# Weighted V of an even and an odd head in one block of matmuls, on the two halves of the array's columns

## What is computed

```python
def dense_causal_attention(q, k, v):
    ...
        s = jnp.einsum('bhqd,bhkd->bhqk', qi, k, preferred_element_type=jnp.float32) * scale
        s = jnp.where(kpos[None, :] <= qpos[:, None], s, -jnp.inf)
        p = jax.nn.softmax(s, axis=-1).astype(v.dtype)
        return jnp.einsum('bhqk,bhkd->bhqd', p, v)
```

## Time and profile before

| | |
|---|---|
| median of three runs | 943.77 us (943.41 to 944.41) |
| the profiled execution | 944.41 us, its span 942.3 us |
| mean granted TensorE clock | 0.992 of full speed |
| busy in the span: PE, DVE, ACT | 898.9 us (95%), 696.2 us (74%), 502.5 us (53%) |
| head loop of layer 0 | about 179.8 to 241.2 us |
| head loop of layer 1 | about 640.1 to 699.9 us |
| L825, layers and heads together | 64 records, 390 ns in the middle |
| L827 | 64 records, 273 ns |

### The profile page before, as it was taken

One profiled execution on the slowest core, in us unless ns is written; L12 is line 12 of the kernel. 1 busy time (PEld: TensorE's weight loads), 2 busy tenths in 40 slices (PEclk: granted clock), 3 DMA queues, 4 the chain that ended last, 5 costly groups with the idle time before them and its releaser, 6 DMA issues.

```text
span 942.3 us, 12772 instructions
## 1 busy us (share of the span) xinstructions
PE 898.9 (95%) x5020; PEld 765.5 (81%) x5020; DVE 696.2 (74%) x1111; ACT 502.5 (53%) x726; POOL 27.8 (3%) x51
## 2 busy tenths in 40 slices
PE   8999989898999999999989998989899999999998
PEld 5788879776987888888868997988689778888886
DVE  5987899688797667685679967986858865575454
ACT  5554977356448443443473569844464763443441
POOL 0010000000000000000001000000000000000000
PEclk9999999999999999999999999999999999999999
DMA  9979825314643857777538973360244556555451
GB/s 376 391 289 382 318 90 179 134 46 179 268 171 142 311 209 270 280 281 281 201 132 340 364 269 134 135 223 2 90 182 179 184 180 230 208 191 187 158 179 45
DMA packets 29581, 198.12 MB, mean 210 GB/s; under 512 B 3281, under 2 KB 3793, under 8 KB 7506
## 3 DMA queue, kind: packets, MB, share of 16 engines
q1 hardware_dynamic: 23474, 155.22, 44.4%
q0 software_dynamic: 5760, 41.95, 11.6%
q10 hardware_dynamic: 288, 0.14, 0.1%
HBM read 196.24 MB, written 1.05 MB: 209 GB/s over the span
## 4 chain that ended last, share of the span: by engine, by line
PE 56%; DVE 29%; ACT 8%; issue 4%; DMA 3%; DVEq 0%; ACTq 0%
PE bank L573 13%; PE bank L575 13%; PE bank L574 13%; DVE w_lo L1352 10%; PE bank L534 3%; PE bank L535 3%; PE bank L536 3%; DMA raw<-in_slabs_dram 3%; DVE score L1544 2%; ACT w_hi L987 2%; DVE acc L1662 2%; DVE front L1359 1%; DVE score L1601 1%; PE bank L922 1%; ACT acc L1234 1%
## 5 line engine op out<-in xcount | busy, mean ns | idle before, releaser
L1352 DVE TENSOR_TENSOR w_lo<-raw,w_hi 128x2048 fp32r<-128x2048 f32 (+2 forms) x146 | 316.6, 2172 | 128.1 <-ACT w_hi L987 126.8
L987 ACT ACTIVATE w_hi<-raw 128x2048 fp32r<-128x2048 f32 (+2 forms) x146 | 264.3, 1811 | 146.8 <-PE bank L575 92.0
L573 PE MATMUL bank<-w_hi,h_hi 128*128 128x512 f32 x536 | 211.3, 394 | 8.2 <-DVE w_lo L1352 5.2
L575 PE MATMUL bank<-w_lo,h_hi 128*128 128x512 f32 x536 | 209.2, 390 | 0.0
L574 PE MATMUL bank<-w_hi,h_lo 128*128 128x512 f32 x536 | 208.9, 390 | 0.0
L573 PEld LDWEIGHTS bank<-w_hi,h_hi 128*128 128x128 f32 x536 | 100.6, 188 | 34.2 <-DVE w_lo L1352 7.7
L575 PEld LDWEIGHTS bank<-w_lo,h_hi 128*128 128x128 f32 x536 | 100.6, 188 | 21.4
L574 PEld LDWEIGHTS bank<-w_hi,h_lo 128*128 128x128 f32 x536 | 100.7, 188 | 20.3
L534 PE MATMUL bank<-h_hi,w_hi 128*128 128x256 f32 x384 | 112.3, 292 | 1.0 <-DVE w_lo L1352 1.0
L535 PE MATMUL bank<-h_lo,w_hi 128*128 128x256 f32 x384 | 109.0, 284 | 0.0
L536 PE MATMUL bank<-h_hi,w_lo 128*128 128x256 f32 x384 | 108.9, 283 | 0.0
(11 more groups left out here) (203 smaller groups left out, 1321.3 us busy)
## 6 DMA issues: line engine op xcount, KB each, us to landing
raw<-in_slabs_dram SPq DMA_DIRECT2D x124, 1024.0 KB, 4.9
front<-in_ada_dram POOLq DMA_DIRECT2D x29, 1024.0 KB, 5.6
acc<-in_ada_dram POOLq DMA_DIRECT2D x11, 1024.0 KB, 7.9
raw<-in_slabs_dram SPq DMA_DIRECT2D x16, 552.0 KB, 7.9
front<-in_ada_dram SPq DMA_DIRECT2D x5, 1024.0 KB, 11.3
raw<-in_slabs_dram SPq DMA_DIRECT2D x6, 768.0 KB, 6.9
proj<-in_ada_dram SPq DMA_DIRECT2D x2, 1024.0 KB, 9.2
x_t<-in_x_dram SPq DMA_DIRECT2D x2, 512.0 KB, 4.7
```

The source lines that it names most:

```text
L573: nc.tensor.matmul(o, hh, wh, start=first, stop=False)
L575: return nc.tensor.matmul(o, hh, wl, start=False, stop=final)
L987: nc.scalar.activation(w_hi[:, n % RING, 0:w], raw[:, n % RING, 0:w], ACT.Copy).then_inc(hi_ready.sem, 1)
L1352: nc.vector.tensor_tensor(w_lo[:, n % RING, 0:w], raw[:, n % RING, 0:w], w_hi[:, n % RING, 0:w], ALU.subtract).then_inc(lo_ready.sem, 1)
```

## The change

PE's `weigh_v` now takes a pair instead of a head. It is called in even steps from 4 on, for pair (n-4)/2: the odd head's V stays in the step where it was, the even head's V moves one step later, next to it. Inside, the four matmuls of two heads alternate: keys 0 to 127 of the even head, of the odd head, then keys 128 to 255 of the even head, of the odd head. Each head writes its own 64 partitions of the bank as before. There is one wait for ACT's copy, that of the odd head, where there were two.

Since an even head's transposed exponentials wait longer for their use, `pt_sb` has four places instead of two, in `acc` columns 1536 to 3071 (the indexer's `relu_b`, finished by then, had the same columns). ACT's copy now waits for V four heads back. Scores, transposes, banks, gate slabs and the order on DVE are as they were.

```diff
-        pt_sb = [acc[:, 2304 + 384 * i:2304 + 384 * (i + 1)] for i in range(2)]
+        pt_sb = [acc[:, 1536 + 384 * i:1536 + 384 * (i + 1)] for i in range(4)]
...
-                def weigh_v(n):
-                    kind, h = HEADS[n]
-                    at = {"a": P * h + A_NOPE, "b": C_BV + HD * h, "c": C_CV + HD * h}[kind]
-                    pair = n // 2
-                    if n % 2 == 0 and pair >= 2:
+                def weigh_v(pair):
+
+                    if pair >= 2:
 
                         pe.wait_ge(y_lo_done.sem, y_lo_done.at(l, pair - 1))
-                    pe.wait_ge(pt_out.sem, pt_out.at(l, n + 1))
-                    r, y = HD * (n % 2), bank[2 + pair % 2]
-                    nc.tensor.matmul(y[r:r + HD, 0:T], proj[:, 0, at:at + HD], pt_sb[n % 2][:, 0:T],
-                                     start=True, stop=False, skip_group_check=True)
-                    nc.tensor.matmul(y[r:r + HD, P:T], proj[:, 1, at:at + HD],
-                                     pt_sb[n % 2][:, T:T + P], start=False, stop=True,
-                                     skip_group_check=True).then_inc(pv_done.sem, 1)
+                    pe.wait_ge(pt_out.sem, pt_out.at(l, 2 * pair + 2))
+                    y, at = bank[2 + pair % 2], []
+                    for n in (2 * pair, 2 * pair + 1):
+                        kind, h = HEADS[n]
+                        at.append({"a": P * h + A_NOPE, "b": C_BV + HD * h, "c": C_CV + HD * h}[kind])
+                    for e in range(2):
+                        nc.tensor.matmul(y[HD * e:HD * (e + 1), 0:T], proj[:, 0, at[e]:at[e] + HD],
+                                         pt_sb[(2 * pair + e) % 4][:, 0:T], start=True, stop=False,
+                                         skip_group_check=True)
+                    for e in range(2):
+                        nc.tensor.matmul(y[HD * e:HD * (e + 1), P:T], proj[:, 1, at[e]:at[e] + HD],
+                                         pt_sb[(2 * pair + e) % 4][:, T:T + P], start=False, stop=True,
+                                         skip_group_check=True).then_inc(pv_done.sem, 1)
...
-                    if n >= 3:
-                        weigh_v(n - 3)
+                    if n >= 4 and n % 2 == 0:
+                        weigh_v((n - 4) // 2)
...
-                        if n >= 4:
-
-                            act.wait_ge(pv_done.sem, pv_done.at(l, n - 3))
-                        nc.scalar.activation(pt_sb[n % 2], bank[6 + n % 2][:, 0:P + T], ACT.Copy)\
+                        if n >= 6:
+
+                            act.wait_ge(pv_done.sem, pv_done.at(l, n - 5))
+                        nc.scalar.activation(pt_sb[(n - 2) % 4], bank[6 + n % 2][:, 0:P + T], ACT.Copy)\
                             .then_inc(pt_out.sem, 1)
```

## The result

| | median of 5 runs, us | lowest to highest | profiled execution: time, span |
|---|---|---|---|
| before, same job | 944.41 | 943.41 to 944.61 | 944.41, 942.3 |
| after | 948.62 | 948.11 to 949.23 | 948.24, 946.2 |

The ratio is 1.0047, 95% interval 1.0032 to 1.0062: slower by 4.2 us where 0.8 was forecast, and above the 947.3 at which the range ended. Lines of the changed kernel: V's two matmuls of a pair are L827 and L831, the maximum L1666, the normalisation L1677, ACT's copy of a head L1250, its y_hi L1255.

The account below looks back on a forecast made before the run. VectorE and ScalarE were taken to bound steps 0 to 11, TensorE step 12 and the last steps. Terms +0.10, +0.05, -0.87, +1.2 and +0.3 gave +0.8 on 943.77: 944.6 us, range 942.6 to 947.3.

Parts of the forecast that it names:

- pair's V block: TensorE's four V matmuls of two heads: halves overlap almost fully, 0.84 us with 0.05 for loading weights; bounds 0.79 and 1.44.
- steps 0 to 11, clock apart: Head loop's first twelve steps, where TensorE waits for VectorE: cheaper V gains the loop nothing.
- step 12, a layer: Pair (8, 9) stands where V(9) stood and still waits for ScalarE's copy of head 9: +0.05 us each layer.
- end of layer 0: Last loop steps of layer 0: the pair now waits for ScalarE's copy of head 15, +0.05 us.
- end of layer 1: Steps 13 to 18 of layer 1: V(12) leaves step 15, so gate slab and turn(15) come earlier, -0.87 us.
- (b): Steps 6 to 7, both layers: longer pause before scores(8) drops the clock, +0.15 us a layer, bounds 0 to 0.5.
- rival 2: Clock also falls at step 11, slowing step 12's gate slab: +1.5 us a layer, 946.1 or 947.6; chance 0.16.
- (a): End of layer 0's loop: pause before turn(15) drops the clock for V and gate slab, +1.2 us (0.5 to 2.2).
- rival 3: In every pair's V block the halves run one after the other: block 1.44 us, +2.4, time 946.4; chance 0.11.
- Rival 1: The clock stays up in the head loops despite longer pauses: -0.7 us, time 943.1; chance 0.20.
- Rival 4: TensorE bounds the head loop more than the chain shows; a third of 11.8 us saved gives 940.7; chance 0.05.

Follow-up runs that it names:

- e6: The changed kernel with filler matmuls on TensorE at the end of steps 6, 7, 11 and, in layer 0, 16: 942.94 us, ratio 0.9988 to before.
- e9: e6 with both heads of a pair on the same half of the array's columns: 945.98 us, ratio 1.0016 to before.
- e3: The kernel before with four places for transposed exponentials instead of two, V still head by head: 943.03 us, ratio 1.0000 to before.
- e2: The kernel before with most of the even heads' V matmuls left out: 946.47 us, ratio 1.0022 to before.
- e4: The changed kernel with both V matmuls of the even head issued first, then both of the odd head: 946.64 us, ratio 1.0034 to before.
- e10: The changed kernel with filler matmuls in two TensorE pauses outside the head loops: 945.73 us, ratio 1.0018 to before.
- e5: e6 without the fillers at step 16 of layer 0: 945.13 us, ratio 1.0004 to before.
- e1: The changed kernel with filler matmuls at the end of steps 6, 11 and, in layer 0, 16: 944.27 us, ratio 1.0007 to before.
- e8: The kernel before with filler matmuls in two TensorE pauses outside the head loops: 941.46 us, ratio 0.9970 to before.

## Why the prediction was wrong

It forecast 944.6, inside 942.6 to 947.3; the run gave 948.62. The mechanisms held, the clock's fall after longer pauses among them; the clock's price did not. Sorted by its own steps, with e6 to take the clock out:

| step of the prediction | forecast | measured |
|---|---|---|
| pair's V block | 0.84 (0.79 to 1.44) | 0.80 |
| steps 0 to 11, clock apart | 0 | 0.00 to 0.01 (e6, scores(13)) |
| step 12, a layer | +0.05 | +0.10, +0.09 |
| end of layer 0 | +0.05 | +0.10 |
| end of layer 1 | -0.87 | -0.83 |
| clock, (b), layer 0 and 1 | +0.15, +0.15 | +0.50, +1.63 |
| clock at step 12 | 0 (rival 2: +1.5) | +1.50 in layer 0, none in layer 1 |
| clock, (a) | +1.2 (0.5 to 2.2) | +2.66 |

The last three rows are after minus e6. They sum to 6.3 where the prediction had 1.5; the rows above them give -0.53 where it had -0.72.

**The block** went to the lower end of its bounds. Loading the second half's weights costs 0.01 at most, where 0.05 was taken. The Trainium skill ("TensorE: Matmul & The Clock Gate", Part 3) has a weight load overlap matmuls in flight only in other row groups. Here both halves use all 128 rows, and 0.80 against e9's 1.42 says that halves of the columns overlap as well; the measurement decides. So rival 3 is out, and the size that it gave to its mechanism, +2.4, is near e9's 1.21 + 1.35 = 2.6.

**Layer 1's end** came as worked out: the gate slab of step 15 stands straight behind turn(13), and turn(15) behind DVE's normalisation. After minus before goes from 1.73 at scores(14) to 0.81 at turn(15). The 0.05 too much at each pair that waits for ACT is there because V starts 0.61 after ACT's copy starts instead of 0.52 (e6 220.27 and 220.88, before 219.92 and 220.44).

**Pauses.** Both were foreseen: 3.36 us before scores(8) where the text said 2.7 to 3, 2.84 before turn(15) where it said 3.0. The clock fell at both.

**The step that failed is the price of a fall.** It was taken from the earlier trace rows as 3.4 us at 1.2 GHz, a loss of at most 1.7. Three of after's four falls in the loops lasted 6.8. One trace of before didn't show that length; the trace of e3, with the same code outside the loops, has it at 124.1 to 130.9, where before's lasted 3.4, so a second execution could have shown it. The bound of 2.2 for (a) had "if it stays low longer" in it, but only by 0.5. At (a) V, the gate slab of step 18 and the start of the branch products are all on PE's path, so most of the 6.8 us counted: 2.66, of at most 3.4. At (b) a slack of 1 us was set against a loss of 1.7 at most. What a fall there costs goes by its moment: in eight loops one of 6.8 us begins near scores(8), and they differ so (e2 against before, the others against e6):

| kernel, layer | clock falls at | scores(8) starts | cost by scores(13) |
|---|---|---|---|
| e4, 1 | 662.1 | 663.17 | 0.42 |
| after, 0 | 199.1 | 200.05 | 0.50 |
| e10, 1 | 661.5 | 662.24 | 0.55 |
| e4, 0 | 201.3 | 201.68 | 0.72 |
| e2, 1 | 662.9 | 663.22 | 0.82 |
| e10, 0 | 200.8 | 199.68 | 1.35 |
| after, 1 | 666.7 | 664.98 | 1.63 |
| e2, 0 | 202.1 | 200.22 | 1.71 |

Where it falls before the wait is over, a part of the low stretch passes over an idle PE; where it falls a microsecond or more after, all of it lies on work. The later it fell, counted from scores(8), the dearer it was, in all eight. No row of before could have told the moment, so with a stretch of 6.8 us (3.4 lost) the bounds of (b) should have been 0 and 3.4 less the slack, 2.4, instead of 0 and 0.5 (the dearest measured is 1.71). Moment matters at (a) too: in e5 the clock fell at 235.4, before turn(15), and cost 2.4; in after at 236.7, with turn(15), and cost 2.66.

**The second error is of the kind of case.** Rival 2, the fall at step 12, happened in layer 0 (219.6 to 223.0), at the place and with the price of +1.5 that it had. It was set up as another case than the forecast, with 0.16, when it is one more fall beside (a) and (b). In e1, e5, e6 two fillers stand there and nothing falls; of the kernels with pairs and without fillers, after has it in layer 0, e4 in layer 1, e10 in neither. So at this place it comes in some executions. Added up with the measured prices from the same job's median of before: 944.41 - 0.53 + 6.3 = 950.2, or 948.7 without the 1.5 of step 12; the median of after is 948.62. Its profiled execution had the 1.5, and the 1.7 of the fall at 170 was absent in it.

**The rest.** Rival 1 is e6 by its condition, if by fillers: 0.7 under before forecast, 0.12% (1.1 us) under it measured, with an interval of 0.01% to 0.22%. Rival 4, PE as the bound, is out by the marks up to scores(8).

What stays open: why a fall lasts 3.4 us in one place and 6.8 in another is seen only as the pattern of e10's halves, with the exception named there; no run varied it alone. In which executions step 12 falls, and at which moment a fall begins, is not explained.

## What to carry to other kernels

Where another engine sets the pace, taking work from TensorE can cost time: look at what its busy share becomes in the stretch before the next work that is on the path, and price a fall of the clock there by all of the path's matmuls that lie in it, for the longest low stretch that several traces of the kernel show (one of before showed only the shorter) and at its least favourable moment. Several such places are to be added, not weighed against each other. If the pause can't be avoided, a few matmuls into a free bank are cheap: 13 in the first loop and 8 in the second (e6) turned a loss of 0.47% into a gain of 0.12%.

## What the runs showed of the hardware

- fp32 matmuls with 64 columns each on the two halves of the array's columns, all 128 rows in both, run at once: 0.80 us a pair, 1.42 on the same half, 0.81 when issued head by head (e4). In e4 matmuls on one half start before matmuls on the other half that were issued ahead of them.
- Less work can be slower by the clock alone: e2 leaves out some 9 us of matmuls and takes 0.22% longer.
- The clock can fall without a long pause: in e1 after waits of 1.44 and 0.99 us with short work between and around them; in e8 after one of 1.16, without the change.
- The low stretches came in two lengths, 3.4 and 6.8 us (but for one at the very end of each trace); the trace of before had only the shorter. At one place, around 125 us, the length differs between executions: 3.4 in before, 6.8 in e3.
- A low stretch of 6.8 us near scores(8) cost between 0.42 and 1.71 us, the more the later it began.
- The kernel before had falls of its own, two a layer outside its loops in the trace; e3, with the same code there, had two in all. Filling the two pauses of the earlier trace rows takes it from 944.40 to 941.46 (e8, ratio 0.9970).
